# Prompt attention of a hybrid decoder step: GpSimd scales the probability rows by the inverse row sums in place of VectorE

## What is computed

```python
def sparse_attend(q, iq, iw, q_pos, k_all, v_all, ik_all, k_pos, topk):
    ...
    qg = q.reshape(bsz, tq, N_KV_HEADS, KV_GROUP, HEAD_DIM)
    logits = jnp.einsum('btngd,btsnd->btngs', qg.astype(jnp.float32), kg.astype(jnp.float32)) * HEAD_DIM ** -0.5
    logits = jnp.where(valid[:, :, None, None, :], logits, -jnp.inf)
    p = jax.nn.softmax(logits, axis=-1)
    o = jnp.einsum('btngs,btsnd->btngd', p.astype(vg.dtype), vg)
    return o.reshape(bsz, tq, ATT_W)
```

## Time and profile before

| | |
|---|---|
| device time, median of 3 runs | 1315.29 us (1311.71 to 1315.46) |
| span of the profiled execution, first to last instruction | 1312.1 us |
| TensorE, matrix products | 1269.6 us busy, 97% |
| VectorE | 879.6 us busy, 67% |
| ScalarE | 679.4 us busy, 52% |
| GpSimd | 699.7 us busy, 53% |
| prompt attention, first transpose to the end of the last group | 343.6 to 486 us |
| the 64 scalings (L2271) on VectorE | 342.7 us to 466.1 us, first and last start |

### The profile page before, as it was taken

The page is one execution under the profiler, slowest core; times in us unless marked ns, Lnnn a source line. Parts: engine busy times, 40 slices in busy tenths (PEclk is TensorE's granted clock), DMA queues, the critical chain, the costliest instruction groups (busy, mean ns, idle before and its releaser), DMA issues.

```text
span 1312.1 us, 25134 instructions
## 1 busy us (share of the span) xinstructions
PE 1269.6 (97%) x9473; PEld 1152.6 (88%) x9473; DVE 879.6 (67%) x1640; ACT 679.4 (52%) x1164; POOL 699.7 (53%) x438
## 2 busy tenths in 40 slices
PE   6899999989899999999999999999999999999998
PEld 4677999877655656999999999999999999999998
DVE  5877889889789948667983455555545453654595
ACT  5657888968887776455352343333334336211115
POOL 0242448990000002457577887888878857765630
PEclk8899999999899999999999999999999999999999
DMA  9722116432101126555321343433434268898633
GB/s 346 278 69 73 50 32 215 156 129 81 52 14 33 36 79 222 169 165 154 111 101 49 114 162 130 163 128 130 171 137 170 82 251 311 311 337 342 249 130 130
DMA packets 127273, 198.85 MB, mean 152 GB/s; under 512 B 16839, under 2 KB 100111, under 8 KB 116656
## 3 DMA queue, kind: packets, MB, share of 16 engines
q1 hardware_dynamic: 127008, 193.01, 42.5%
q10 hardware_dynamic: 144, 4.23, 0.8%
HBM read 144.07 MB, written 53.18 MB: 150 GB/s over the span
## 4 chain that ended last, share of the span: by engine, by line
PE 66%; DVE 15%; ACT 6%; DVEq 4%; issue 3%; ACTq 2%; SPq 2%; DMA 1%; POOL 0%
PE ps L3468 30%; PE ps L3488 15%; DVE junk L2043 3%; ACT junk L1319 3%; PE ps L3175 2%; ACTq L1321 2%; PE ps L3163 2%; PE ps L3332 2%; PE ps L3334 2%; PE ps L3333 2%; DMA ada_shift<-in_ada_w 1%; PE ps L3152 1%; DVEq L2594 1%; PE ps L3285 1%; DVE lg L2260 1%
## 5 line engine op out<-in xcount | busy, mean ns | idle before, releaser
L1012 POOL TENSOR_TENSOR wL<-wraw,wH 128x1024 fp32r<-128x1024 f32 x28 | 70.0, 2503 | 262.7 <-ACT wH L1312 262.4
L3488 PE MATMUL ps<-input,down_H 128*128 128x258 f32 x1120 | 180.7, 283 | 2.8 <-DVE acc L2742 1.5
L3488 PEld LDWEIGHTS ps<-input,down_H 128*128 128x128 f32 x1120 | 154.4, 190 | 3.5 <-issue 2.5
L3468 PE MATMUL ps<-comb,opH 128*128 128x258 f32 x960 | 154.4, 283 | 0.0
L1135 POOL TENSOR_TENSOR opL<-wsum,opH 128x512 fp32r<-128x512 f32 x80 | 124.5, 1565 | 36.9 <-ACT opH L1660 33.5
L1660 ACT CAST opH<-wsum 128x512 fp32r<-128x512 f32 x80 | 49.6, 621 | 167.6 <-PE ps L3468 114.3
L3468 PEld LDWEIGHTS ps<-comb,opH 128*128 128x128 f32 x960 | 132.7, 190 | 0.0
L3468 PE MATMUL ps<-h2H,opH 128*128 128x258 f32 x640 | 129.0, 283 | 0.3 <-DVE h2L L2599 0.3
L3468 PE MATMUL ps<-h2H,opL 128*128 128x258 f32 x640 | 129.0, 283 | 0.0
L3468 PE MATMUL ps<-h2L,opH 128*128 128x258 f32 x640 | 128.6, 282 | 0.0
L2742 DVE TENSOR_TENSOR acc<-ps,acc 128x516 f32<-128x516 f32 x112 | 76.4, 693 | 62.6 <-PE ps L3488 62.0
(11 more groups left out here) (523 smaller groups left out, 3477.1 us busy)
## 6 DMA issues: line engine op xcount, KB each, us to landing
down_inputs<-staged SPq DMA_DIRECT2D x35, 1032.0 KB, 4.5
input<-down_inputs SPq DMA_DIRECT2D x35, 1032.0 KB, 6.7
adb<-in_ada_w SPq DMA_DIRECT2D x8, 2048.0 KB, 8.4
wraw<-in_w_out SPq DMA_DIRECT2D x24, 512.0 KB, 4.3
raw<-in_w_gate SPq DMA_DIRECT2D x10, 1024.0 KB, 6.3
raw<-in_w_up SPq DMA_DIRECT2D x10, 1024.0 KB, 5.1
down_block<-in_w_down SPq DMA_DIRECT2D x5, 2048.0 KB, 10.9
x_feature_major<-x0T ACTq DMA_DIRECT2D x1, 4128.0 KB, 15.6
```

The costliest lines, as they stand in the source:

```text
L1012: pool.tensor_tensor(lo[:], raw_[:], hi[:].bitcast(F32), ALU.subtract).then_inc(s_wL, 1)
L3468: ins = mm(ps[:, sum_bank(v, p) + h, 0:HC], weight[s][:, k, :], token[:, k, h * HC:(h + 1) * HC], start=begins, stop=ends, skip_group_chec ...
L3488: ins = mm(ps[:, 2 * m + h, 0:HC], weight[:, f, cc], tok[:, f, part, h * HC:(h + 1) * HC], start=(f == 0 and weight is hi and part == 0), ...
```

## The change

The scaling of the rows by `pinv` moves from VectorE's loop to GpSimd, ahead of its `low(u)`. VectorE keeps the inverse; the semaphore `s_pn` now tells that the four inverses of a group are there, and a second count, on a semaphore that was in use once before (`s_diw`, for the decode queries), tells the scaled heads. GpSimd waits once for each group, then scales its four heads in order. TensorE waits in the first step of a group ahead of each head's transpose for that head. VectorE's `drain` between inverse and scaling goes.

```diff
+            def scaled_probs(n):
+
+                pool.wait_ge(s_pn, n + 1)
+                for g in range(GRP * n, GRP * (n + 1)):
+                    buf = lg[g % NLG][:, 0:P * (tile_of(n) + 1)]
+                    pool.tensor_scalar(buf, buf, pinv[:, g % NLG:g % NLG + 1], None, ALU.mult).then_inc(s_psc, 1)
+
+            for n in range(NG):
+                scaled_probs(n)
             for u in range(NU_LRU, U_FFN):
                 low(u)
...
-                V.reciprocal(pinv[:, s:s + GRP], psum_r[:, s:s + GRP])
-
-            def scaled_probs(g):
-                buf = lg[g % NLG][:, 0:P * (tile_of(g // GRP) + 1)]
-                V.tensor_scalar(buf, buf, pinv[:, g % NLG:g % NLG + 1], None, ALU.mult).then_inc(s_pn, 1)
+                V.reciprocal(pinv[:, s:s + GRP], psum_r[:, s:s + GRP]).then_inc(s_pn, 1)
...
             inverse(0)
-            dve.drain()
-            for h in range(GRP):
-                scaled_probs(h)
             for n in range(NG):
                 new = n + AHEAD
                 if n + 1 < NG:
                     inverse(n + 1)
-                    dve.drain()
                 for step in range(GRP):
...
-                    if step < 2 and n + 1 < NG:
-                        scaled_probs(GRP * (n + 1) + 2 * step)
-                        scaled_probs(GRP * (n + 1) + 2 * step + 1)
...
-                if k == 0:
-                    pe.wait_ge(s_pn, GRP * (n + 1))
                 pe.wait_ge(s_bte, item - 1)
                 for h in range(GRP):
+                    if k == 0:
+                        pe.wait_ge(s_psc, after(GRP * n + h + 1))
                     ins = tr(ps[:, 4 + item % 2, h * P:(h + 1) * P],
                              lg[(GRP * n + h) % NLG][:, k * P:(k + 1) * P], ident)
```

More of the change, by code:

```diff
@@ L544, in build @@
         s_diq = sem("decode_index_query")
-        s_diw = sem("decode_index_query_laid_out")
+        s_diw = sem("decode_index_query_laid_out_then_probs_scaled")
         s_dnk = sem("decode_new_key_product_then_block12_taken")
@@ L575, in build @@
         s_ex = sem("exponentials_ready")
-        s_pn = sem("probs_scaled")
+        s_pn = sem("inverse_sums_ready")
         s_bt = sem("bank_transposed")
@@ L631, in build @@
         s_s1, s_s2, s_s3 = s_csi, s_rb, s_dg
+        s_psc = s_diw
         s_c11, s_c22, s_c12, s_c21 = s_exl, s_nsp, s_dnk, s_dnr
```

## The result

The changed kernel takes 1345.74 us in the median (1342.6 to 1347.59) against 1315.38 us for the kernel before (1311.71 to 1316.61): a ratio of 1.0235 with a 95% interval of 1.022 to 1.0251, or about 30.4 us more. Forecast were 19.3 us more. The sign was right and the size was not: 1.0235 times the 1315.3 us of before is 1346.2 us, just over the upper end of the range, and the median itself lies 0.3 us inside it. Runs of one kernel can differ by several us along with their granted clock (0.977 in the two faster runs of the change, 0.971 and 0.972 in the others), so such differences between single runs mean nothing.

A forecast was written before the change was run, and what follows sets the result against it. TensorE and VectorE, both nearly full, were taken to bound the prompt attention, closed into a ring by GpSimd's scalings: 10.9 (group 15 late) + 3.3 (contention) + 5.1 (clock) = 19.3 us, 1315.3 + 19.3 = 1334.6; range 1314 to 1346.

The forecast's parts named there:

- The dear form: GpSimd's one-operation multiply by a column of factors: 0.30 us + 2.49 ns a column, 2.85 us at 1024 columns.
- The ring: Prompt attention: transposes, logits of n+2, mask, VectorE's tail, inverse, four GpSimd scalings, next transposes; group 15 10.9 us late.
- Rival (a): GpSimd scales 1024 columns in 1.2 us, as in its two-operation row; links fall to TensorE's work: 1307, chance 0.13.
- Rival (b): Prompt attention: more slack than counted, gain on VectorE and loss on GpSimd cancel: 1315, chance 0.06.
- Rival (c): Prompt attention: groups wait for GpSimd's scalings but TensorE's clock does not drop: 1326 to 1330, chance 0.22.
- the term of the clock: TensorE's waits ahead of groups 6, 8 and 10 each cost 1.7 us at half clock: 5.1 us, bounds 0 and 5.1.
- the forecast's links: Times between starts of even groups in prompt attention, such as 15.7 us for 4 to 6, 24.4 for 8 to 10.
- both terms: The two smaller additions in prompt attention: 3.3 us for VectorE held up beside GpSimd, 5.1 us for TensorE's clock.
- The contention: Turns 9, 11 and 13: two-input VectorE instructions take 0.9 us longer while GpSimd scales: +3.3 us, bounds 0 and +3.3.
- rows 8: Profile before: a two-input VectorE instruction took 2.16 us beside a GpSimd scaling, 1.28 a moment later; GpSimd's kept its length.
- rival (e): Exclusive port: each two-input VectorE instruction waits for the GpSimd scaling under way: 1340, up to 1345, chance 0.12.
- (b) to (e): The cases that set the range, 1314 to 1346 us, holding 0.82; (d), the forecast itself, 1331 to 1339, has 0.42.

The follow-up runs named there:

- the kernel with fewer filling products: The change plus 84 dummy TensorE products ahead of its waits for scaled heads, in place of 106 in a first filled kernel (1338.28 us): 1336.59 us.

## Why the prediction was wrong in size, and what it had right

**Right.** TensorE and VectorE are nearly full and swing, so relieving VectorE gives 8 us and not 30 (6.7 measured, between 4 and 8). The dear form: 2845 ns for 2.85 us. The ring as the mechanism, with everyone waiting in turn, and little changed behind the stage: 840.9 against 839.7 us. Rival (a), the cheap form, was sized at 1307, and its kernels ran at 1309.3 and 1310.8; its turning point of about 8 us a group lies between the measured 7.0 and 9.7. Rival (b), gain and loss cancel, falls: the wait for GpSimd is 25.0 us. Rival (c), the ring without clock drops, falls with the clock rows above.

**The step that failed** is the term of the clock, "All three gaps are longer than the one with a drop, so I take 5.1". TensorE lost 12.6 us to the low clock ahead of the inverse sums of group 15, in place of 5.1, and this is most of the miss.

**The place of the miss.** When the inverse sums of the even groups and of the last one are formed, in us: by the forecast's links alone (the start of the group less its scalings, plus 0.15; group 2 starts at 351.3 + 1.1), after, and in the kernel with fewer filling products:

| group | forecast | after | filled, fewer |
|---|---|---|---|
| 2 | 348.8 | 350.2 | 350.2 |
| 4 | 359.4 | 362.2 | 360.9 |
| 6 | 373.9 | 378.2 | 377.5 |
| 8 | 391.5 | 397.5 | 396.2 |
| 10 | 414.6 | 425.4 | 421.2 |
| 12 | 436.5 | 450.6 | 444.1 |
| 14 | 459.9 | 477.6 | 469.8 |
| 15 | 472.1 | 490.0 | 482.2 |

At group 15 the forecast with both terms was 472.1 + 3.3 + 5.1 = 480.5, and 490.0 came: 9.5 us. The links from one row of the table to the next can be freed of the clock in two ways, and both are estimates from the traces: take from the link of after the TensorE time that the low clock took in it; or take the link of the filled kernel, less what products that outlast the scaling held up (in group 4 the fourth transpose came 2.0 us late by this, in group 6 0.8).

| link | forecast | after | less the clock | filled | less late products |
|---|---|---|---|---|---|
| 2 to 4 | 10.6 | 11.9 | 10.2 | 10.7 | 10.7 |
| 4 to 6 | 14.5 | 16.1 | 14.3 | 16.6 | 14.6 |
| 6 to 8 | 17.6 | 19.3 | 17.6 | 18.7 | 17.9 |
| 8 to 10 | 23.1 | 27.9 | 24.6 | 25.0 | 25.0 |
| 10 to 12 | 21.9 | 25.3 | 22.7 | 23.0 | 23.0 |
| 12 to 14 | 23.4 | 27.0 | 25.3 | 25.6 | 25.6 |

The two ways agree within 0.5 us. Up to group 8 the forecast's links are right, and the miss there is a start 1.4 us late and the clock. By the first way the clock is 7.5 of the 9.5 us and all else 2.0; by the second 5.5 and 4.0.

**The term of the clock** was mis-sized in its count and its length. It looked at one gap per group, at groups 6, 8 and 10, and at one length of drop, 3.4 us. But TensorE waits for each head by itself, so a gap comes in pieces, and the clock fell behind the pieces too: at about 355, 369 and 386 us, behind three waits each in groups 2, 4 and 6, none of them longer than 1.21 us (0.5 to 0.6 us each in group 2, where the forecast had no gap). In the 3.09 us ahead of group 8's last head and the 2.96 us ahead of group 10's it fell within the wait, at 406.5 and 433.8 us, and stayed down twice as long, 6.8 us. A sixth drop followed the 3.13 us ahead of group 12, where the forecast had no gap either. The link from 8 to 10 shows what that costs: from 406.84 to the inverse at 425.36 are 18.5 us where 15.7 were taken over from before, and the clock took 3.3 of them.

**The links** are short of the filled kernel by 8.5 us and 1.4 at the start (group 2, which the forecast had 0.3 earlier than the kernel before although its scalings were dearer) and 0.2 at the end, 10.1 in all, of which 3.3 were allowed for as contention. Of these, 2.8 us are the late products. Most of the rest is the contention below.

**The contention** was sized at 3.3 us, and 4.3 came, the other way round. Forecast from rows 8 was a VectorE instruction held up by 0.9 us beside a GpSimd one of usual length. In the trace after, one scaling in each of the groups 8, 10 and 12 is held up by a VectorE scan (shortest, median and longest of the group's scalings, the first row with one of group 9; then VectorE beside group 12's last):

```profile
L1116 POOL TENSOR_SCALAR lg<-lg,pinv x5: 1877/1883/3437, 397.8 to 406.8; 128x640 f32<-128x640 f32 x5
L1116 POOL TENSOR_SCALAR lg<-lg,pinv x4: 2203/2208/3312, 425.6 to 432.2; 128x768 f32<-128x768 f32 x4
L1116 POOL TENSOR_SCALAR lg<-lg,pinv x4: 2522/2526/4417, 450.9 to 458.4; 128x896 f32<-128x896 f32 x4
```

```profile
458.23 2.28 DVE L2241 TENSOR_TENSOR_SCAN xr<-decay,xr 128x1024 f32<-128x1024 f32 x1
460.58 0.75 DVE L2243 TENSOR_TENSOR xr<-xr,decay 128x8 f32<-128x8 f32 x1
461.55 1.23 DVE L2247 TENSOR_TENSOR gel<-gel,xr 128x1032 f32<-128x1032 f32 x1
```

The scan had begun 0.2 us before the scaling and kept its 2.28 us (it took the same at 420.92, with GpSimd idle); the scaling that began at 458.4 took 4.42 in place of 2.53 us, 1.9 more, nearly the whole scan. In groups 8 and 10 it was 1.6 and 1.1 us, with scans that had begun at 402.81 and 431.19, and were of usual length. The four scalings thus took 9.0, 9.9 and 11.9 us where the forecast, whose price for one was a little dear, had 7.6, 8.8 and 10.1: 4.3 us, and all of it on the path, since TensorE waits for the fourth head. With 1.4 at the start, 4.3 in place of 3.3 and 12.6 in place of 5.1, the forecast's 472.1 comes to 490.4, against 490.0 measured.

The Trainium skill, "SBUF — State Buffer", section "Who interferes with whom", says that the order of issue decides which engine blocks. The three held scalings agree with it. It does not hold throughout here: each of the three scans began while the scaling before was still under way, and neither was longer for it; and the product with two inputs at 461.55 took 1.23 us beside the long scaling, as at 423.65 with GpSimd idle. The small product at 460.58 took 0.75 us where the same line took 0.17 at 423.27, alone. No VectorE instruction of this stage waited for a whole scaling, the longest hold of a large one being 0.7 us (2.00 at 486.55, where the same one took 1.28 before). So rival (e) falls, in its direction and its price. That GpSimd can be the one held up stood in the trace of before, in the view that rows 8 are from: its instruction on 8 columns took 1.03 us at 276.74, beside VectorE, and 0.33 at 252.28.

**What the range missed.** It was built from (b) to (e) one at a time, with 1345 as the end of (e). The clock term had no upper end of its own above 5.1 us, though the trace showed only one priced drop. With 12.6 us in its place the forecast would have been 1342.1. That the measured time lies so near the upper end that (e) had set is luck: (e) is not what happened.

## What to carry to other kernels

Look for the cheapest form of an instruction before an engine is judged: a one-operation multiply by a column on GpSimd costs 2.5 times the two-operation one, and a product with 1.0 turned 30 us of loss into 5.5 us of gain. Where work moves to a slower engine inside a ring, compare its time in a row with the faster engines' turn: below it the move was free here, beyond it every microsecond was paid in each link, and part of it once more in TensorE's clock. Where an engine waits for the pieces of a work one by one, count the short waits too when you ask what its clock does. Work that stands ahead of a wait can be its cover: to move the wait forward cost 8 to 12 us in kernels in which nothing else had changed.

## What the runs showed of the hardware

- GpSimd's multiply by a per-partition column in 32-bit floats: 2846 ns for 1024 columns with one operation, 1118 ns with a second one (times 1.0), 1119 with plus 0.0, 1197 with a second column, and 1894 as a product of two tensors with the column broadcast. That more operations cost less was not expected.
- TensorE's granted clock fell behind several waits of 0.5 to 1.2 us in a row (0.57 in 355 to 359, 368.5 to 372.5 and 386 to 390 us), not only behind single ones of 2.6 us and more. In the change, between 350 and 560 us, each drop to half the clock lasted 3.4 or 6.8 us. Products that do nothing, put into these waits, brought back 9 us; the same kind of products without waits cost 0.21 us each (22.2 us for 106).
- A scan on VectorE of 2.28 us stretched the scaling that GpSimd began during it from 2.53 to 4.42 us, and two others by 1.6 and 1.1 us. The scans kept their length, though each began while a scaling was under way; so did a two-input product of 1.23 us beside the long scaling.
